# Five matmuls for a weight block instead of six, in a two-layer decoder step

## The reference, cut to what matters

```
D_MODEL = 1024; SEQ = 512; DEC_BATCH = 8; D_FF = 2816; SGU_WIDTH = 2048
# layer 0: z = gelu(h @ w_in); u, v = split(z); v = rms_norm(v)
#          s = (causal 128x128 mix of v) + b_s;  m = (u * s) @ w_out
# layer 1: latent attention over a shared latent (w_dkv, w_dq, w_uq, w_uk, w_uv, w_o)
def conv_ffn(h, conv_prev, w_up, conv_w, conv_b, w_down):      # in both layers
    a = h @ w_up
    ap = concatenate([conv_prev, a], axis=1)
    c = conv_b + ap[:, 0:t] * conv_w[0]
    for k in range(1, 3):
        c = c + ap[:, k:k + t] * conv_w[k]
    g, u = split(c, 2, axis=-1)
    return (gelu(g) * u) @ w_down, ap[:, t:]
```

## Time and profile before

| | |
|---|---|
| median of 3 runs | 1464.67 us (1464.09 to 1467.34) |
| span of the profiled execution (first to last instruction) | 1461.2 us |
| granted TensorE clock, mean over the span | 0.985 of full |
| PE busy | 1409.3 us, 96% |
| DVE busy | 894.1 us, 61% |
| ACT busy | 536.8 us, 37% |
| POOL busy | 175.0 us, 12% |
| DMA | 138.20 MB, mean 95 GB/s |

### The profile page before, as it was taken

How to read it: one execution, slowest core, us unless ns; L and a number is a source line. 1 busy time by engine, 2 the same in 40 slices (tenths; PEclk the granted TensorE clock), 3 DMA queues, 4 the chain that set the end, 5 groups by cost and what they waited for, 6 DMA issues and landing times.

```text
span 1461.2 us, 30495 instructions
## 1 busy us (share of the span) xinstructions
PE 1409.3 (96%) x11815; PEld 1329.9 (91%) x11815; DVE 894.1 (61%) x1518; ACT 536.8 (37%) x870; POOL 175.0 (12%) x329
## 2 busy tenths in 40 slices
PE   6999999998999999999999989998999999999997
PEld 5999999998999999999989855657999999999997
DVE  4444664227888888633375686464578888884334
ACT  4545443236222223333464212344543222223334
POOL 1000000000222222100001020100012322321000
PEclk9999999999999999999999999799999999999999
DMA  7332222321332232233425463101223233222331
GB/s 232 103 86 73 73 75 82 91 87 48 97 100 87 86 100 80 78 96 89 119 69 187 176 248 125 48 1 34 83 60 100 86 94 92 86 77 88 92 90 65
DMA packets 224370, 138.20 MB, mean 95 GB/s; under 512 B 12620, under 2 KB 220674, under 8 KB 223256
## 3 DMA queue, kind: packets, MB, share of 16 engines
q1 hardware_dynamic: 219688, 112.38, 26.5%
q0 software_dynamic: 4224, 24.62, 4.5%
q10 hardware_dynamic: 384, 0.16, 0.1%
HBM read 133.83 MB, written 3.67 MB: 94 GB/s over the span
## 4 chain that ended last, share of the span: by engine, by line
PE 91%; DVE 5%; ACT 2%; issue 1%; DMA 1%; SPq 0%; DVEq 0%; ACTq 0%
PE psum L659 76%; PE psum L1054 2%; PE psum L1183 1%; PE psum L1160 1%; PE psum L1037 1%; PE psum L718 1%; PE psum L1015 1%; PE psum L818 1%; PE psum L1163 1%; DVE ut L1686 1%; DVE x L1689 1%; DVE kt L1978 1%; DMA xn<-in_x_prompt 1%; PE psum L1172 1%; DVE wl L1647 1%
## 5 line engine op out<-in xcount | busy, mean ns | idle before, releaser
L1647 DVE TENSOR_TENSOR wl<-ws,wh 128x1024 fp32r<-128x1024 f32 x217 | 265.8, 1225 | 336.5 <-ACT wh L1243 173.5
L659 PE MATMUL psum<-xh,wh 128*128 128x260 f32 x2064 | 426.6, 285 | 11.0 <-DVE xl L1666 6.2
L659 PE MATMUL psum<-xh,wl 128*128 128x260 f32 x2064 | 421.5, 283 | 0.0
L659 PE MATMUL psum<-xl,wh 128*128 128x260 f32 x2064 | 420.6, 283 | 0.0
L659 PEld LDWEIGHTS psum<-xh,wh 128*128 128x128 f32 x2064 | 320.9, 189 | 14.3 <-issue 13.5
L659 PEld LDWEIGHTS psum<-xh,wl 128*128 128x128 f32 x2064 | 320.6, 189 | 0.0
L659 PEld LDWEIGHTS psum<-xl,wh 128*128 128x128 f32 x2064 | 320.0, 188 | 0.4
L1243 ACT ACTIVATE wh<-ws 128x1024 fp32r<-128x1024 f32 x144 | 152.2, 1057 | 319.1 <-PE psum L659 319.1
L659 PE MATMUL psum<-acth,wh 128*128 128x260 f32 x704 | 144.3, 284 | 0.0
L659 PE MATMUL psum<-acth,wl 128*128 128x260 f32 x704 | 143.2, 282 | 0.0
L659 PE MATMUL psum<-actl,wh 128*128 128x260 f32 x704 | 143.0, 282 | 0.0
(11 more groups left out here) (283 smaller groups left out, 1812.9 us busy)
## 6 DMA issues: line engine op xcount, KB each, us to landing
ws<-in_w_up SPq DMA_DIRECT2D x88, 512.0 KB, 3.8
ws<-in_w_in_a SPq DMA_DIRECT2D x32, 512.0 KB, 4.1
ws<-in_w_down SPq DMA_DIRECT2D x32, 384.0 KB, 3.4
ws<-in_w_down SPq DMA_DIRECT2D x32, 320.0 KB, 3.1
ws<-in_w_out_a SPq DMA_DIRECT2D x16, 512.0 KB, 3.9
ws<-in_w_o SPq DMA_DIRECT2D x8, 512.0 KB, 4.6
xn<-in_x_prompt SPq DMA_DIRECT2D x4, 512.0 KB, 10.1
ws<-in_w_dq SPq DMA_DIRECT2D x4, 512.0 KB, 4.6
```

Of the source, the lines that this page charges most:

```text
L659: mm = pe.matmul(psum[:, 2 * slot + b, 0:HB], w, r[:, k, b * HB:(b + 1) * HB], start=st, stop=en)
L1647: dve.tensor_tensor(low_, ws[:, slot4, :], f32(high), ALU.subtract).then_inc(w_low, 1)
```

## The change

Tokens are split into parts of WA = 284 and WB = 236. High and low activations lie in one tile (`xhl`, `ushl`, `acthl`, `cqhl`), so that one matmul with the high weights can stream both the high and the low of the second part, 2 x 236 = 472 columns. It writes wh·xh to the second bank's first 236 columns and wh·xl, apart, to the 236 after them. The first part is at the end of the first bank, so that both parts together are still 520 neighbouring columns. A block is now 472 + 284 + 284 + 284 + 236 columns, 1560 as before.

This is done in 139 units of 8 blocks (14 of v, 16 of u, 14 of wo, 84 of up, 4 of dq, 7 of o) and in 14 down tiles of 22 blocks, 1420 blocks in all; what is run in halves, the third unit of kv and uq keep six matmuls, now of 284 and 236 columns. Where a block has five, the low sum has to be added: ACT copies it out of PSUM (`copy_low`, 236 columns, ahead of `wh` in most stages) and DVE adds it into the second part (`fold`, 236 columns, PSUM to PSUM) after it has read out the first part. In v the first two units are run in halves and have no fold. In wo, down and o, `raw` on ACT now waits for the fold.

The first convolution step (bias and first weight) moves from DVE to ACT. It waits there for the read-out, for the state from POOL and for the product of the pair before; DVE's second step waits for it (`conv_first`). `cc` moves to the place of the temporaries.

```diff
-HB = T // 2
+WA, WB = 284, 236
         def acc(slot):
-            return psum[:, 2 * slot:2 * slot + 2, 0:HB]
+            return flat[:, 1024 * slot + 512 - WA:1024 * slot + 512 + WB]
+        def part(slot, h):
+            return psum[:, 2 * slot + 1, 0:WB] if h else psum[:, 2 * slot, 512 - WA:512]
+        def part_and_low(slot):
+            return psum[:, 2 * slot + 1, 0:2 * WB]
+        def low_part(slot):
+            return psum[:, 2 * slot + 1, WB:2 * WB]
...
# PE, product
+                if apart:
+                    pe.matmul(part_and_low(slot), hw, rhl[:, :, k, HALF[1]], start=first, stop=False, skip_group_check=True)
                 for w, r, st, en in ((hw, rh, first, False), (hw, rl, False, False), (lw, rh, False, last)):
                     for b in parts:
-                        mm = pe.matmul(psum[:, 2 * slot + b, 0:HB], w, r[:, k, b * HB:(b + 1) * HB], start=st, stop=en)
+                        if not (apart and b and w is hw):
+                            mm = pe.matmul(part(slot, b), w, r[:, HALF[b]], start=st, stop=en, skip_group_check=apart and b == 1)
...
# ACT
+            def copy_low(done, slot, b):
+                act.wait_ge(mm_done, done)
+                act.activation(lows[:, b, :], low_part(slot), ACT.Copy).then_inc(low_copied, 1)
...
# ACT, up tile, after wh and acth
+                    act.wait_ge(evac_up, NF * l + q + 1)
+                    act.wait_ge(state_in, NF * l + q + 1)
+                    wait(act, prod_done, KF * l + j)
+                    act.activation(cc[:, u % 2, :], ab[:, u % 2, 0:CW_], ACT.Identity, bias=pt[:, bass.ds(C_CB + l * NF + f, 1)],
+                                   scale=pt[:, bass.ds(conv_rows(l, 0) + f, 1)]).then_inc(conv_first, 1)
...
# DVE
+            def fold(stage, t, slot, b):
+                dve.wait_ge(low_copied, FOLD[stage] + t + 1)
+                dve.tensor_tensor(part(slot, 1), part(slot, 1), lows[:, b, :], ALU.add).then_inc(folded, 1)
...
# DVE, gate tile (v, dq and up alike)
-                dve.tensor_tensor(halves(ut[:, 0, :]), acc(u % 2), halves(r1[:, :]), ALU.mult).then_inc(evac_sgu, 1)
+                dve.tensor_tensor(ut[:, 0, HALF[0]], part(u % 2, 0), r1[:, HALF[0]], ALU.mult)
+                fold("u", j, u % 2, u % 2)
+                dve.wait_ge(folded, FOLD["u"] + j + 1)
+                dve.tensor_tensor(ut[:, 0, HALF[1]], part(u % 2, 1), r1[:, HALF[1]], ALU.mult).then_inc(evac_sgu, 1)
...
# DVE, up tile
-                    dve.tensor_scalar(cc[:, b, :], ab[:, b, 0:CW_], w[0], bias, ALU.mult, ALU.add).then_inc(conv_step, 1)
-                    dve.wait_ge(conv_step, 2 * Q + 1)
+                    dve.wait_ge(conv_first, Q + 1)
```

More of the change, by code:

```diff
@@ L650, in _, with product @@
         def _(pe):
-            def product(n, slot, nslot, k, kk, rh, rl, first, last, parts=(0, 1)):
+            def product(n, slot, nslot, k, kk, rhl, first, last, parts=(0, 1), apart=False):
+                rh, rl = rhl[:, 0, k, :], rhl[:, 1, k, :]
                 if nslot == 2:
@@ L671, in unit, with first_units @@
                         between[kk]()
-                    mm = product(n, slot, nslot, k, koff + kk, rh, rl, first and kk == 0, last and kk == len(ks) - 1)
+                    mm = product(n, slot, nslot, k, koff + kk, rhl, first and kk == 0, last and kk == len(ks) - 1, apart=apart)
                 mm.then_inc(mm_done, 1)
-            def first_units(n, rh, rl, sem, before_half, between):
+            def first_units(n, rhl, sem, before_half, between):
                 pe.wait_ge(w_low, n + 2)
@@ L823, in gate_unit @@
                 pe.wait_ge(evac_sgu, U_U + j - 1)
-                unit(U_U + j, weight_slot(U_U + u), u % 2, range(KD), xh, xl, True, True, between=between)
+                unit(U_U + j, weight_slot(U_U + u), u % 2, range(KD), xhl, True, True, between=between)
             def mix_early():
@@ L871, in wo_tile @@
                 for half in range(1 if last else 2):
-                    unit(U_WO + 2 * t + half, weight_slot(U_WO + half), e, range(half * KD, (half + 1) * KD), ush, usl, half == 0, half == 1,
-                         ready=[(usl_ready, 0)] if first else None)
+                    unit(U_WO + 2 * t + half, weight_slot(U_WO + half), e, range(half * KD, (half + 1) * KD), ushl, half == 0, half == 1,
+                         ready=[(usl_ready, 0)] if first else None, apart=not last)
                     if first and half == 0:
@@ L915, in down @@
                     for w, (k0, kc) in enumerate(DN_SPLIT[:3] if last else DN_SPLIT):
-                        unit(U_DN[l] + 4 * t + w, weight_slot(U_DN[l] + w), e, range(k0, k0 + kc), acth, actl, w == 0, w == 3,
-                             ready=[(actl_ready, KF * l)] if first else None)
+                        unit(U_DN[l] + 4 * t + w, weight_slot(U_DN[l] + w), e, range(k0, k0 + kc), acthl, w == 0, w == 3,
+                             ready=[(actl_ready, KF * l)] if first else None, apart=not last)
                     if last:
@@ L920, in down @@
                         pe.wait_ge(csn_ready, l + 1)
-                        last_unit(U_DN[l] + 4 * t + 3, range(k0, k0 + kc), acth, actl, False, g)
+                        last_unit(U_DN[l] + 4 * t + 3, range(k0, k0 + kc), acthl, False, g)
                 pe.wait_ge(evac_up, NF * (l + 1) - 1)
@@ L940, in _ @@
             mlp(0)
-            locked_units(U_KV, xkh, xkl, xkl_ready, 0, "m_ffn0", "x2")
-            unit(U_KV + 2, weight_slot(U_KV + 2), 2, range(KD), xkh, xkl, True, True)
+            locked_units(U_KV, xkhl, xkl_ready, 0, "m_ffn0", "x2")
+            unit(U_KV + 2, weight_slot(U_KV + 2), 2, range(KD), xkhl, True, True, apart=False)
             for t in range(KQ):
@@ L950, in _ @@
                     pe.wait_ge(evac_dq, t - 1)
-                unit(U_DQ + t, weight_slot(U_DQ + t), (3 + t) % 2, range(KD), xh, xl, True, True, ready=[(xl_ready, XB[2])] if t == 0 else None)
+                unit(U_DQ + t, weight_slot(U_DQ + t), (3 + t) % 2, range(KD), xhl, True, True, ready=[(xl_ready, XB[2])] if t == 0 else None)
                 if t == 0:
@@ L1276, in square @@
                 sq_slot_free(name, t)
-                out = sq[:, slot, :]
-                act.activation(halves(out) if len(src.shape) == 3 else out, src, ACT.Square).then_inc(sq_done, 1)
+                act.activation(sq[:, slot, 0:T], src, ACT.Square).then_inc(sq_done, 1)
             def update(p, name, m):
@@ L1374, in _ @@
                 if u >= 2:
+                    copy_low(U_V + u + 1, 2 if u == 2 else 1, u % 2)
                     ahead_static(U_V + u)
@@ L1464, in down @@
                     t = 2 * i + e
+                    last = isinstance(t, int) and t == KD - 1
                     for w in range(4):
+                        if w == 3 and not last:
+                            copy_low(U_DN[l] + 4 * t + 4, e, e)
                         if guard:
@@ L1813, in wo @@
                     for half in range(2):
+                        if half and not (isinstance(t, int) and t == KD - 1):
+                            fold("wo", t, e, e)
                         ahead(U_WO, 4, i, 2 * e + half)
@@ L1893, in down @@
                     for w in range(4):
+                        if w == 3 and not (isinstance(t, int) and t == KD - 1):
+                            fold(f"dn{l}", t, e, e)
                         if guard:
@@ L2134, in _ @@
             for t in range(KD):
+                if t < KD - 1:
+                    fold("o", t, t % 2, t % 2)
                 ahead_static(U_O + t)
```

212 lines of the change are left out of this document (123 added, 89 removed).

## The result

| | before | after |
|---|---|---|
| median of the runs (6 and 6) | 1465.95 us | 1470.8 us |
| span of the profiled execution | 1461.2 us | 1469.6 us |
| granted TensorE clock, mean | 0.985 | 0.984 |
| PE busy | 1409.3 us | 1415.3 us |
| DVE busy | 894.1 us | 908.2 us |

The account below looks back on a forecast made before the run. PE, busy 96% of the span, was taken as the bound. Blocks -46.5, gate tiles +4.4 and passages +2 gave -40.1 us: span 1461.2 to 1421.1, with 3.5 around it 1424.6, said as 1425; range 1413 to 1440.

Parts of the forecast that it names:

- 430 ns at 512 float32 columns: Block cost on PE: with a long stream the load is hidden and an instruction's price is 3 ns.
- 116 ns with 8 columns: Block cost on PE: matmuls streaming next to nothing show a weight load takes at least 112 to 116 ns.
- 216.7 ns at half clock: Block cost on PE: at 1.2 GHz the 260 columns alone set the pace; at full clock some 12 ns are extra.
- only columns count: Rival on block cost: the extra is a slower stream of this format; gain 3.9 us less 6.4, 1467; chance 0.09.
- The load starts with the matmul before: Block cost on PE: a matmul takes the longer of its stream and its load, about 120 ns, hiding 260 columns.
- The term: PE's gain per block, 0.722 to 0.686 us, 0.036 less; over 1292 blocks -46.5 us.
- Gate tiles: u stage: copy and fold lengthen the ACT and DVE chain to 7.34 us against 7.05 a tile; +4.4 us.
- dq's late end: End of dq: PE waits for a chain whose last tile gets 0.9 us longer; with v to u, +2 us.
- v just hidden, wo and down at nothing: v's chain of 5.37 us stays below PE's 5.49, by 0.1; wo, down and o lose nothing to the later `raw`.
- Up hidden: Up, 84 units: PE still sets the pace, 10.98 us a pair against DVE's 9.9; full gain of 24.2 us.
- The fallback at narrow widths: Rival: 236 columns fall back to float32's two passes, 0.39 us against 0.12; +387 us, about 1850; chance 0.05.
- 3.5 us around the span: Last step of the sum: the median lies 3.5 us above the profiled span, turning 1421.1 into 1424.6.

Follow-up runs that it names:

- The widths: Two runs of matmuls alone, decoder left out, fp32r at many widths: 236 columns 111.7 ns, 260 120.1, 284 130.8.

## Why the prediction was wrong

The step that failed is the first: what the 120.3 ns of a 260-column matmul are. I took them for a weight load that the stream hides under, and the five wider matmuls were to share fewer loads. Each piece of the argument had another reading, and the runs show it:

- *430 ns at 512 float32 columns, "the price of an instruction is 3 ns".* Right in size (the line has 4), but a row of another format says nothing of the columns of this one. The widths show 0.446 ns a column here and 0.417 in bf16.
- *116 ns with 8 columns.* A floor does exist, 111 to 112 ns, but it is reached only below about 248 columns. Only the narrow part touches it, and there it costs (2.7 ns) instead of giving.
- *216.7 ns at half clock.* It says that the extra is gone at 1.2 GHz. I read that as the load's being hidden; a column price that is not tied to the clock fits as well. That was the rival "only columns count", dismissed with "nothing in the trace has another length to exclude it", which should have raised its chance of 0.09, not lowered it.
- *The load starts with the matmul before, the next matmul 0.12 behind.* The rows give the order in time and don't say which of the two is the longer.

So the block came out at 0.719 us by the widths, 0.720 in up and 0.717 in down (4.29 + 4.30 + 3.60 + 3.58 us for 22 blocks), not at 0.686. The term was -2 us by the widths (1.6 ns by 1292 blocks), not -46.5. The rival that had this gave 1467. That is 2.3 us above its 1464.67; measured were 4.85 above 1465.95. That it came so near is in part luck. What it lacked: of the gain for the saved instruction (4 ns a block) the floor at 236 eats 2.7, and the stages that keep six matmuls, now of unequal parts, pay a little more (0.3 of uq's 0.8).

Behind that step things held:

- *Gate tiles.* 6.44 + 0.26 + 0.64 = 7.34 us forecast, 7.325 measured; ACT's `wh` stopped waiting for PE, and PE waits for `vn`, as written. The kernels with and without copy and fold show that this is the cause. That the size fits to 0.02 is in part luck: the read-out grew by 0.51 us, not 0.64, so the chain is 6.44 + 0.27 + 0.51 = 7.22, and the waits of the copy for PE in some tiles make up the rest. Over the 16 tiles with the passage from v it is +4.5 us once the half-clock stretch is taken off, where 4.4 and part of the 2 for passages were said: 3.7 in the last twelve units and 0.8 in the first.
- *dq's late end.* It shows in the first unit of uq: 8.98 us where it was 8.40, and 8.49 in the kernel without folds. PE waits 0.3 us there for the last `sq`, for which it didn't wait before. The two passages are 0.8 + 0.6 us, where 2 were said.
- *v just hidden, wo and down at nothing.* v -0.1, wo +0.1, down -1.4 us.
- *Up hidden.* PE sets the pace, at 5.76 us a unit. I had 0.2 us of room a pair against a PE of 10.98; against the real 11.52 it is wide, 0.7 to 1.0 at each read-out. The step on ACT took 0.84 us, not 0.73. The gelu that was to hold up the odd tile's copy was through 0.28 us before PE's unit ended. Putting the step back on DVE shows what the room is worth: DVE then lags and some 4 us a layer come due.
- *The fallback at narrow widths* did not come: 236 columns take 112 ns.
- *3.5 us around the span.* The six executions of the kernel after have 1.8 us between span and time, and those of the kernel before beside the first experiments 1.8 to 2.9. So the last step of the sum was 1 to 2 us too high; it changes nothing in the outcome.

The rule of the Trainium skill ("TensorE: Matmul & The Clock Gate", section "Back-to-back issue gap"), which I set aside since the trace's 120.3 did not agree with its 110.8 ns, forecast no gain worth having, and that was the outcome. Its gap, N / 2.4 + 2.5 ns, agrees with this case's bf16 rows (110.9 ns at 260 columns, where it gives 110.8; 215.9 at 512, where it gives 215.8) and disagrees with the fp32r rows mostly by a factor in the column (0.446 against 0.417 ns), not by a load. The disagreement should have been a reason to ask what is special to the format before reading it as a load.

## What to carry to other kernels

Before merging matmuls to save instructions, find the price of a column in the kernel's own format: if the time goes as the columns, fewer and wider instructions give back only a few ns each, and a split into unequal parts loses on whichever part falls under the floor. Where the trace holds a single width, the slope and the intercept can't be told apart, and a forecast that lives on that difference needs equal weight on both. What a merge adds to the other engines must be walked through stage by stage: here the same fold was free in up and cost 0.3 us a tile in u, where it stood in a chain that had 0.6 us of slack.
